# The opening of an S5 block rebuilt: B and C loaded in their natural layout and turned on TensorE, E built on GpSimd from early on, a second F group ahead of U, and the V loop taken two pairs at a time

## The reference

```
def s5_mixer(u, lam_re, lam_im, log_dt, b_re, b_im, c_re, c_im, d_skip, w_glu):
    ug = uf.reshape(bsz, seqlen, SSM_GROUPS, SSM_GROUP)
    dt = jnp.exp(log_dt.astype(f32))[:, None]
    mag = jnp.exp(lr * dt)
    ab_re = mag * jnp.cos(li * dt)
    ab_im = mag * jnp.sin(li * dt)
    ...
    coef_re = (nr * lr + ni * li) / den
    coef_im = (ni * lr - nr * li) / den
    bb_re = coef_re[..., None] * br - coef_im[..., None] * bi
    bb_im = coef_re[..., None] * bi + coef_im[..., None] * br
    bu_re = jnp.einsum('blgh,gph->blgp', ug, bb_re)
    bu_im = jnp.einsum('blgh,gph->blgp', ug, bb_im)
    ...
    _, _, xs_re, xs_im = lax.associative_scan(combine, (a_re, a_im, bu_re, bu_im), axis=1)
    y = (jnp.einsum('blgp,ghp->blgh', xs_re, c_re.astype(f32))
         - jnp.einsum('blgp,ghp->blgh', xs_im, c_im.astype(f32)))
    y = y.reshape(bsz, seqlen, D_MODEL) + d_skip.astype(f32) * uf
    y = jax.nn.gelu(y).astype(u.dtype)
    a, g = jnp.split(y @ w_glu, 2, axis=-1)
    return a * jax.nn.sigmoid(g)
```

## Time and profile before

| what | value |
|---|---|
| runs of the kernel before | 2005.61, 2001.52, 2005.14 us; median 2005.14 |
| span of the profiled execution | 1998.3 us |
| busy share of the span | PE 96%, VectorE 47%, ScalarE 38%, GpSimd 55% |
| chain that ended last | PE 86%, VectorE 6%, ScalarE 2%, GpSimd 2%, issue 2%, DMA 1%, SyncE 1% |
| costliest group | L2598, L2599, L2600 PE, gb<-xh,wh and the like, x1856 each, about 600 us each |
| w_ada blocks | 48 of 1 MB, median 5.5 us from issue to landing |

### The profile page before, as it was taken

The page is one execution under the profiler, slowest core; times in us unless marked ns, Lnnn a source line. Parts: engine busy times, 40 slices in busy tenths (PEclk is TensorE's granted clock), DMA queues, the critical chain, the costliest instruction groups (busy, mean ns, idle before and its releaser), DMA issues.

```text
span 1998.3 us, 31484 instructions
## 1 busy us (share of the span) xinstructions
PE 1912.5 (96%) x13077; PEld 1644.2 (82%) x13077; DVE 934.3 (47%) x1688; ACT 755.8 (38%) x1212; POOL 1108.0 (55%) x611
## 2 busy tenths in 40 slices
PE   8989999989999999899999999999999999989997
PEld 5578999878887788687778888888788988979997
DVE  7956641364935774732453111114386846372112
ACT  4343553332325422722323222222446435434443
POOL 6435997563535443343443444444468745757885
PEclk8999999989999999999999999999999999989999
DMA  6866776664122132124333323323634421655653
GB/s 165 239 215 225 256 230 219 239 216 156 62 76 64 33 126 64 32 64 137 127 107 126 95 79 121 104 63 110 209 116 128 159 85 54 204 196 174 189 173 98
DMA packets 289490, 276.60 MB, mean 138 GB/s; under 512 B 19802, under 2 KB 276324, under 8 KB 289092
## 3 DMA queue, kind: packets, MB, share of 16 engines
q1 hardware_dynamic: 286804, 271.42, 43.0%
q10 hardware_dynamic: 2192, 2.77, 0.4%
q0 software_dynamic: 352, 0.40, 0.1%
HBM read 266.70 MB, written 4.19 MB: 136 GB/s over the span
## 4 chain that ended last, share of the span: by engine, by line
PE 86%; DVE 6%; ACT 2%; POOL 2%; issue 2%; DMA 1%; SPq 1%; DVEq 0%; ACTq 0%; POOLq 0%
PE gb L2598 19%; PE gb L2599 18%; PE gb L2600 18%; PE gb L1757 3%; PE gb L1755 3%; PE gb L1756 3%; PE gb L1482 3%; PE gb L1483 3%; PE gb L1484 3%; POOL wl L2585 1%; PE mb L1208 1%; PE mb L667 1%; PE gb L667 1%; PE mb L1275 1%; DMA raw<-in_w_ada 1%
## 5 line engine op out<-in xcount | busy, mean ns | idle before, releaser
L2585 POOL TENSOR_TENSOR wl<-raw,wh 128x1024 fp32r<-128x1024 f32 (+3 forms) x448 | 977.8, 2201 | 797.0 <-ACT wh L819 796.7
L819 ACT CAST wh<-raw 128x1024 fp32r<-128x1024 f32 (+3 forms) x452 | 419.4, 937 | 680.8 <-PE gb L2600 399.7
L2598 PE MATMUL gb<-xh,wh 128*128 128x256 f32 (+1 forms) x1856 | 603.4, 325 | 11.0 <-DVE xl L1158 6.9
L2599 PE MATMUL gb<-xl,wh 128*128 128x256 f32 (+1 forms) x1856 | 599.5, 323 | 0.0
L2600 PE MATMUL gb<-xh,wl 128*128 128x256 f32 (+1 forms) x1856 | 599.4, 323 | 0.0
L2598 PEld LDWEIGHTS gb<-xh,wh 128*128 128x128 f32 x1856 | 351.8, 190 | 47.2 <-issue 14.6
L2600 PEld LDWEIGHTS gb<-xh,wl 128*128 128x128 f32 x1856 | 351.8, 190 | 27.6
L2599 PEld LDWEIGHTS gb<-xl,wh 128*128 128x128 f32 x1856 | 351.9, 190 | 27.2
L1755 PE MATMUL gb<-fhh,wh 128*128 128x512 f32 (+1 forms) x352 | 118.4, 336 | 0.0
L1757 PE MATMUL gb<-fhh,wl 128*128 128x512 f32 (+1 forms) x352 | 117.9, 335 | 0.0
L1756 PE MATMUL gb<-fhl,wh 128*128 128x512 f32 (+1 forms) x352 | 117.9, 335 | 0.0
(11 more groups left out here) (475 smaller groups left out, 3028.7 us busy)
## 6 DMA issues: line engine op xcount, KB each, us to landing
raw<-in_w_in SPq DMA_DIRECT2D x62, 1024.0 KB, 5.4
raw<-in_w_ada SPq DMA_DIRECT2D x48, 1024.0 KB, 5.5
raw<-in_w_ffn SPq DMA_DIRECT2D x44, 1024.0 KB, 5.2
raw<-in_mlp_w SPq DMA_DIRECT2D x32, 1024.0 KB, 5.6
raw<-in_w_ffn SPq DMA_DIRECT2D x16, 768.0 KB, 4.3
raw<-in_w_ffn SPq DMA_DIRECT2D x16, 640.0 KB, 4.1
raw<-in_ssm_w_glu SPq DMA_DIRECT2D x8, 1024.0 KB, 6.9
raw<-in_w_out SPq DMA_DIRECT2D x8, 1024.0 KB, 4.8
```

What stands on the lines that cost most here:

```text
L819: nc.scalar.copy(split_half(wh, p, j, h), raw_half(p, it, j, h)).then_inc(hi_ready, 1)
L2585: nc.gpsimd.tensor_tensor(split_half(wl, p, j, h), raw_half(p, it, j, h), split_half(wh, p, j, h).bitcast(F32), ALU.subtract)\
L2598: nc.tensor.matmul(o, H[:, k, :], XH, start=st, stop=False)
L2599: nc.tensor.matmul(o, H[:, k, :], XL, start=False, stop=False)
```

## The change

**Loads.** B comes by GpSimd's queue as two transfers of 32 partitions (`Bq`), C by SyncE's queue as two transfers (`cnat`). The gain, as 32 rows (`wq`), is made into diagonals (`wdiag`, one GpSimd operation of 32x1024), and 64 small products with them turn and weigh B at once, into PSUM banks 0 and 3. 32 small products turn C. x by chunk position is loaded to where the ring will be, so that the ring's first transfer waits for all eight copies of it in place of U's transposes.

**TensorE.** `warm(21)` becomes `warm(3)`; B, C, raw U, x in two halves, the vectors, `warm(3)`, w_ada blocks 0 and 1, the norm factor, blocks 2 and 3, then the loop. The loop handles two pairs per turn (16 turns), and holds six w_ada blocks in place of four, the first half of the K products (turn 9), the skip products and half of K's way back (turn 11). Twelve w_ada products in place of ten stand before y; those among y are at y3 and y5 (before: y0, y1, y3, y6).

**VectorE.** No product with the gain; F group 1 stands ahead of U; one `e_beside` in place of two, and no `e_last`, no `gate_lo`. **ScalarE.** Ct is copied between the two halves of x by group, two pairs' w1 in one copy. **GpSimd.** `wdiag` and `Db` early, E as soon as the powers and Ct are there, the chunk powers behind E's second quarter, seven halves of E in place of five, and all low halves of w_glu.

The core of the diff (pure moves of code and new buffer addresses are left out):

```diff
-        h32 = at("h32", [NCH, CH, D], F32, offset=arena1)[0]
-        xg = at("xg", [NCH, GROUPS, CH, GH], F32, offset=raw_at)[0]
-        xnat = at("xnat", [P, 2, D], F32, offset=toep_at)[0]
-        cnat = at("cnat", [P, 2, 4, P], F32, offset=toep_at + 8192)[0]
+        h32 = at("h32", [NCH, CH, D], F32, offset=raw_at)[0]
+        xg = at("xg", [NCH, GROUPS, CH, GH], F32, offset=toep_at)[0]
...
-        EARLY_ADA, EARLY_GLU = 10, 2
+        EARLY_ADA, EARLY_GLU = 12, 2
...
-                sp.wait_ge(s_U, 1)
+                sp.wait_ge(s_xg, CH)
...
-            sp.wait_ge(s_lnat, 16 * 3)
             xc = A["x"][0].rearrange("(c j) d -> j c d", j=CH)
-            for ri, name in enumerate(("ssm_b_re", "ssm_b_im")):
-                bn = A[name][0].rearrange("(q g) p h -> (g p) q h", g=2)
-                for r in range(2):
-                    sp.dma_start(Bn[:, ri, 16 * r:16 * r + 16, :], bn[:, 16 * r:16 * r + 16, :]).then_inc(s_Bn, 16)
-            rowg = A["norm_mix"][0].rearrange("(q g h) -> g q h", g=2, h=GH)
-            for g in range(2):
-                sp.dma_start(gain[64 * g:64 * g + 64, :, :], rowg[g].partition_broadcast(64)).then_inc(s_Bn, 16)
+            for ri, name in enumerate(("ssm_c_re", "ssm_c_im")):
+                sp.dma_start(cnat[:, ri, :, :], A[name][0].rearrange("(r g) h p -> (g h) r p", g=8)).then_inc(s_cnat, 16)
...
-            sp.wait_ge(s_ss, 1)
-            sp.wait_ge(s_ct5, 1)
+            sp.wait_ge(s_U, 1)
...
+            for j in range(4):
+                x_by_group(j)
...
+            act.wait_ge(s_ct5, 1)
+            act.wait_ge(s_vz, 2)
+            nc.scalar.copy(Ct[:, 0, :, 0:GH], gb[:, 1, :].rearrange("p (q h) -> p q h", h=GH)).then_inc(s_Ctc, 1)
+            nc.scalar.mul(Ct[:, 1, :, 0:GH], gb[:, 2, :].rearrange("p (q h) -> p q h", h=GH), -1.0).then_inc(s_Ctc, 1)
+            for j in range(4, CH):
+                x_by_group(j)
             act.wait_ge(s_xnat, 16)
+            act.wait_ge(s_Bt, 1)
...
-            act.wait_ge(s_xt, 1)
-            nc.scalar.copy(x[:, :, 0:SEQ], gb[:, :, :].rearrange("p b (k t) -> p (b k) t", k=2)).then_inc(s_x1, 1)
+            for i in range(2):
+                act.wait_ge(s_xt, i + 1)
+                nc.scalar.copy(x[:, 4 * i:4 * i + 4, 0:SEQ],
+                               gb[:, 1:3, :].rearrange("p b (k t) -> p (b k) t", k=2)).then_inc(s_x1, 1)
...
+            for b in range(PAIRS // 2):
+                act.wait_ge(s_w1t, b + 1)
+                if b >= 2:
+                    act.wait_ge(s_w1u, b - 1)
+                nc.scalar.copy(w1[:, 2 * (b % 2):2 * (b % 2) + 2, :, :],
+                               gb[:, 1 + b % 2, :].rearrange("p (a r m) -> p a r m", a=2, r=2)).then_inc(s_w1, 1)
+                if b % 4 == 0 and b:
+                    v_copy(b // 4 - 1)
+                if b == K_FIRST:
+                    kt_copy(0)
...
+            pool.dma_start(wq[:, :], A["norm_mix"][0].rearrange("(q n) -> q n", q=PAIRS)).then_inc(s_wq, 16)
+            for ri, name in enumerate(("ssm_b_re", "ssm_b_im")):
+                pool.dma_start(Bq[:, ri, :, :, :], A[name][0].rearrange("(q g) p h -> q g p h", g=2)).then_inc(s_Bq, 16)
...
+            pool.wait_ge(s_const, 16)
+            pool.wait_ge(s_wq, 16)
+            nc.gpsimd.tensor_tensor(wdiag[:, :, :, :].rearrange("q g h n -> q (g h) n"),
+                                    ident[0:PAIRS, 0:PAIRS].unsqueeze(1).to_broadcast([PAIRS, 2 * GH, PAIRS]),
+                                    wq[:, :].unsqueeze(2).to_broadcast([PAIRS, 2 * GH, PAIRS]), ALU.mult).then_inc(s_gd, 1)
+            nc.gpsimd.memset(sc[:, :, :], 0.0).then_inc(s_vz, 1)
+            nc.gpsimd.memset(zeros[:, :, :], 0.0).then_inc(s_vz, 1)
...
+            pool.wait_ge(s_pw, 1)
             pool.wait_ge(s_Ctc, 2)
-            pool.wait_ge(s_Bb, 1)
-            pool.wait_ge(s_U, 1)
             e_half(0, 0)
+            e_half(0, 1)
+            pool.sem_inc(s_E, 1)
             pool.wait_ge(s_th, 1)
             for s_ in range(2):
                 o = V_C + 8 * s_
                 pstep(g_.tensor_scalar(sc[:, :, 30 + s_], sc[:, :, 30 + s_], 0.5, 0.5, ALU.mult, ALU.add))
                 pstep(g_.tensor_tensor(sc[:, :, 30 + s_], sc[:, :, 30 + s_], vecs[:, o:o + 8], ALU.mult))
             pool.sem_inc(s_sc, 1)
-            e_half(0, 1)
-            pool.sem_inc(s_E, 1)
             e_half(1, 0)
             e_half(1, 1)
             pool.sem_inc(s_E, 1)
+            chunk_powers()
             e_half(2, 0)
+            e_half(2, 1)
+            pool.sem_inc(s_E, 1)
+            e_half(3, 0)
             pool.sem_inc(s_E, 1)
...
-                        if p is p_glu and it == 0 and j < EARLY_GLU:
-                            continue
-                        if p is p_glu and it == 0 and j == EARLY_GLU:
-                            pool.wait_ge(w_ready, 2 * EARLY_GLU)
...
-            warm(21, 3)
...
+            warm(3, 2)
+            pe.wait_ge(s_Bq, 16 * 2)
+            pe.wait_ge(s_gd, 1)
+            for ri in range(2):
+                for h in range(GH):
+                    for g in range(2):
+                        ins = nc.tensor.matmul(gb[64 * g:64 * g + 64, 3 * ri, PAIRS * h:PAIRS * h + PAIRS],
+                                               Bq[:, ri, g, :, h], wdiag[:, g, h, :], start=True, stop=True)
+            ins.then_inc(s_Bt, 1)
+            pe.wait_ge(s_cnat, 16 * 2)
+            of_parity = ident.rearrange("p (q g h) -> p g q h", q=4, g=2)
+            for ri in range(2):
+                for r in range(8):
+                    for g in range(2):
+                        ins = nc.tensor.matmul(gb[64 * g:64 * g + 64, 1 + ri, 64 * r:64 * r + 64],
+                                               cnat[:, ri, r, :], of_parity[:, g, :, :], start=True, stop=True)
+            ins.then_inc(s_ct5, 1)
...
+            pe.wait_ge(s_Ctc, 2)
+            pe.wait_ge(s_xnat, 16)
+            for i in range(2):
+                if i:
+                    pe.wait_ge(s_x1, 1)
+                for k in range(4):
+                    for a in range(2):
+                        ins = nc.tensor.transpose(gb[:, 1 + k // 2, (k % 2) * 256 + a * P:(k % 2) * 256 + a * P + P],
+                                                  xnat[:, a, (4 * i + k) * P:(4 * i + k) * P + P], ident)
+                ins.then_inc(s_xt, 1)
+            pe.wait_ge(s_vnat, 16 * NVEC)
+            pe.wait_ge(s_x1, 2)
+            for a in range(4):
+                ins = nc.tensor.transpose(gb[:, 1, a * P:a * P + P], vnat[:, a, :], ident)
+            ins.then_inc(s_vt, 1)
+            warm(3, 2)
+            pe.wait_ge(s_vc, 1)
+            pe.wait_ge(s_Bb, 1)
+            pe.wait_ge(s_sc, 1)
+            for n in range(2):
+                ada_block(pe, n)
             pe.wait_ge(s_small, 32)
             pe.wait_ge(s_chk, 1)
             for a in range(2):
+                ins = nc.tensor.matmul(gb[:, 1, GH * a:GH * a + GH], const[:, REP:CHK], chk[:, a, :], start=True, stop=True)
             ins.then_inc(s_fp5, 1)
+            for n in range(2, 4):
+                ada_block(pe, n)
+            pe.wait_ge(s_fac, 1)
...
+            pe.wait_ge(s_Uc, 1)
+            for b in range(PAIRS // 2 + 1):
+                if b == 12:
+                    for n in range(8, 10):
+                        ada_block(pe, n)
+                if b < PAIRS // 2:
+                    w1_transposes(b)
+                if b:
+                    v_products(b - 1)
+                if b in (2, 5, 7, 10):
+                    ada_block(pe, {2: 4, 5: 5, 7: 6, 10: 7}[b])
+                if b == K_FIRST:
+                    pe.wait_ge(s_Vc, 2)
+                    k_products(0)
+                if b == K_FIRST + 2:
+                    skip_products()
+                    k_back(0)
+            pe.wait_ge(s_w1, PAIRS // 2)
             k_products(1)
+            ada_block(pe, 10)
             k_back(1)
+            ada_block(pe, 11)
+            warm(8, 1)
...
-                late = ((0,), (1,), (), (2,), (), (), (3,), ())[d]
+                late = ((), (), (), (0,), (), (1,), (), ())[d]
...
-            dve.wait_ge(s_Bn, 16 * 6)
+            dve.wait_ge(s_Bt, 1)
+            Bn = [gb[:, 3 * ri, :].rearrange("p (h q) -> p q h", q=PAIRS) for ri in range(2)]
             cf = [sm[:, k, :].unsqueeze(2).to_broadcast([P, PAIRS, GH]) for k in (15, 17)]
-            cmul(Bb[:, 0, :, :], Bb[:, 1, :, :], Bn[:, 0, :, :], Bn[:, 1, :, :], cf[0], cf[1],
-                 tE[:, 0:PAIRS * GH].rearrange("p (q h) -> p q h", h=GH))
-            step(v.tensor_tensor(Bb[:, :, :, :], Bb[:, :, :, :],
-                                 gain[:, :, :].unsqueeze(1).to_broadcast([P, 2, PAIRS, GH]), ALU.mult))
+            cmul(Bb[:, 0, :, :], Bb[:, 1, :, :], Bn[0], Bn[1], cf[0], cf[1], tB[:, :, :])
...
+            f_group(1)
             dve.wait_ge(s_U, 1)
             dve.wait_ge(s_fac, 1)
             dve.wait_ge(s_sk, 1)
```

(15 more changed lines are left out.)

244 lines of the change are left out of this document (92 added, 152 removed).

## The result

| what | before | changed |
|---|---|---|
| median of 19 runs each | 2005.61 us | 2015.96 us |
| lowest and highest | 1999.95, 2010.2 | 2005.59, 2020.02 |
| ratio, 95% interval | | 1.0045, 1.0031 to 1.0058 |
| span of the profiled execution | 1998.3 | 2004.1 |
| first of the long products at | 124.6 | 128.1 |

The forecast was 2019.5 (1999 to 2026). The new runs split: four at 2005.6 to 2007.5, fifteen at 2011.2 to 2020.0. The profiled execution took 2005.88 and is one of the four, so its trace shows a mild form. By the same 1.8 the profiled execution of before (span 1998.3) took about 2000.1, my estimate, also at the low end of its kernel's 19 runs.

A forecast was written before the change was run, and what follows sets the result against it. TensorE, busy 96%, bounds the kernel, its long products starting at 124.6 us. Loop start +21, loop -4.6 and +8.0, y 17.5 later but 19.75 long: products at 139.2, +14.5, so 2019.5 against 2005.1; range 1999 to 2026.

The forecast's parts named there:

- largest term: VectorE's coefficients in the opening: six operations held by GpSimd's E, so that they end at 31 us, not at 20.
- the two waits that it blamed: GpSimd's E waited for U's transposes and Bb; without these waits E was to hold VectorE's operations before the scan.
- B's way: Start of the opening: spread-gain wait 1.69 and gain product 1.36 go, 3.05 us gained; B turned at 13 to 16.
- Powers: VectorE's opening: `wdiag` and two Db operations on GpSimd hold the powers, ending at 18 us (bounds 12 to 19.1).
- Coefficients: VectorE after the powers: E starts at 18 us too, six operations are held, ending at 31, not 20.
- rsqrt: VectorE behind F group 0: comes at 44.5, held by GpSimd's E, passes at about 55; about 8 us more.
- Loop: 16 turns of 1.15 us for 32 of 0.72: -4.6; added w_ada, K and skip work: +8.0; last V copy at 99.2.
- Scan to y: Between loop and y: scan and lags take 19.8 us to 119.2; y at 119.4, 17.5 later than before.
- y: Stage before the long products: 22.75 less 3.10 (w_ada wait) and 1.4 (clock), plus 1.5 (gelu holds), 19.75 us.
- C comes late: Rival: Ct copied at 20.5, coefficients pass before E; products at 122.2, 2003 us (2001 to 2006), chance 0.19.
- The clock falls within the loop: Rival: the loop's turns wait for ScalarE and the clock drops, up to 18.4 us more; chance 0.03.
- Sums: Opening's added instants: F group 0 at 44.5 from Bb at 36 and 8.1; F group 1 at 63.5 after rsqrt at 55.

The follow-up runs named there:

- e12: The changed kernel with GpSimd's E again waiting for Bb and U's transposes, silu(c) between its first halves: median 2014.3 us, 1.0045 of the kernel before.
- e1: The changed kernel run and profiled again, nothing altered: median 2012.1 us, 1.0049 of the kernel before.
- e7: The changed kernel with the four low halves of w_glu's first blocks back on VectorE: median 2012.8 us, 1.0036 of the kernel before.
- e6: The changed kernel with K's first half and way back, skip products and w_ada blocks 8 and 9 behind the loop: median 2012.7 us, 1.0043 of before.
- e2: The changed kernel with two GpSimd memsets moved behind the powers and Db's two products on VectorE behind F group 1: median 2019.8 us, 1.0068 of before.
- e9: The changed kernel with GpSimd's memsets behind the powers and Db's products behind silu(c): median 2010.3 us, 1.0025 of the kernel before.
- e3: The changed kernel with TensorE fillers, one more ahead of B and seven between C and U's transposes: median 2015.2 us, 1.0043 of the kernel before.
- e4: The changed kernel with the edits of e2 and e3 together: median 2024.3 us, 1.0086 of the kernel before.
- e10: The kernel of e9 with rsqrt's running values in PSUM and more TensorE fillers before the loop: median 2010.4 us, 1.0024 of the kernel before.
- e11: The kernel of e10 with e6's edit and three quarters of E's second half on VectorE: median 2005.0 us, 0.9999 of the kernel before.

## Why the prediction was right, and where its steps were not

The sign and the range were right, and so was the kind of cause: VectorE held by GpSimd. The place and the sizes were not. 14.5 us were forecast; the profile of 2005.9 shows 3.5 up to the products, the medians 10.4. That the forecast came as near as it did is in good part luck. Its path (`chk` at 55, U at 65.8, y at 119.4) occurs in no profile of the changed kernel's opening: `chk` came at 38.5 to 49.4, U at 50.1 to 60.1, and y at 105.8 to 113.1. Its largest term was absent in two of four, and e12, which puts back the two waits that it blamed, keeps the loss. Terms that it left out stood in their place.

- **B's way.** 13 to 16 was forecast, 17.2 measured: the 64 products took 7.31, above the 6.8 that was to be the upper bound. The 3.05 gained was never seen, since the coefficients came later than B.
- **Powers.** Bounds 12 to 19.1, taken 18, measured 20.1, outside. The two Db holds were there (2.36 and 2.35), but `wdiag` was priced alone, at 2.35: with three memsets it held one TENSOR_SCALAR for 4.37 us. Memsets were priced at nothing, and operations with one SBUF input were left out.
- **Coefficients.** "Six of these are held; they end at 31": in the first profile none was, Ct being copied at 21.9, beyond my bound of 20.5, and they end at 22.1. This step failed, and it is 9 us of the forecast path. It is a matter of chance: E began at 22.08 in the first profile and at 26.91 in e1, and no coefficient was held; it began at 21.36 in e7, and two were (3.5 us); at 21.18 in e6, and three were (5.7 us).
- **rsqrt.** "Comes at 44.5, passes at about 55", some 8 us of holds: in the first profile it came at 35.4 and found a gap. It was held for 3.8 us in e1 and, with `chk`, for 5.6 in e6, and also in e2, e9 and e12. So the mechanism is right, and the price of 8 too high.
- **The norm factor.** Not in my sum at all: silu(c) and w_ada stand ahead of it on TensorE, and most of what precedes them ran at half clock, so that it was ready at 47.7. Before it was ready at 38.4.
- **Loop.** Turn 1.15 forecast, 1.18 measured (transposes at 54.29, 55.47 and 56.64). Last V copy 3.4 us later than the loop's start would give; 5.8 measured. The excess is a wait of 1.77 us, since ScalarE copied K ahead of `w1`, and one for a w_ada block.
- **Scan to y.** 19.8 and y right behind the lags: 19.6 and 0.1.
- **y.** 19.75 forecast, 22.3 measured. The w_ada wait went as said. In its place stand waits of 0.59 and 1.97 us for held gelu operations, the longest 2.68, and the lower clock came back behind them (0.50 from 128 to 130, first products 0.21 us apart): 1.5 was priced, 2.6 and the clock of about 1.4 were found.
- **Rivals.** The first profile is the rival "C comes late", stage by stage: `chk` 37 forecast and 38.5 found, U 48 and 50.1, y 102.4 and 105.8; its sum missed the loop's and y's excess. Its ground, that TensorE "has little to do there, as in 31 to 37", misreads: TensorE was busy for 6.00 of those 6.00 us, with narrow products at 0.50. "The clock falls within the loop" had 0.03 and was seen in e2, e3, e4 and e6. Whether it lies behind the runs at 2016 to 2020 of the changed kernel was not seen, as none of those is profiled.
- **Sums.** F group 0 at 44.5 and F group 1 at 63.5 are each 0.4 over what their terms give (36 + 8.1, 55 + 8.1). Nothing hangs on it.

What the runs show of the cause: with GpSimd's early work out of the way about 4 to 6 of the 10 us come back (e9, e10), and all of it with K behind the loop and E shared as before on top (e11). What each of these parts is worth by itself, and what lengthens the rest of the program in some executions, stays open.

## What to carry to other kernels

Before work is moved to GpSimd, list what VectorE does beside it and whether its operands lie in PSUM; a small operation of the critical chain in SBUF costs as much as the GpSimd operation it meets, and when that meeting hangs on a landing DMA, the kernel can get a spread as well as a loss (`chk` at 38.5 to 49.4 in four profiles of one opening; e9 took 4 to 6 us back by order alone). Work moved out of a loop shortens the loop by its full length, but the path only up to the next thing that waits for that work (in e6 8 us in the loop, 2.7 up to y). Profile more than one execution before an instant is taken for the kernel's. Do not leave TensorE idle ahead of a chain of small matmuls: a gap of 6.5 us cost 5.7 more behind it, and fillers took that back.

## What was not expected of the hardware

- Memsets hold VectorE too, and single-input operations from SBUF to SBUF are held: a COPY of 0.27 us lasted 5.10, a TENSOR_SCALAR of 0.18 lasted 4.37, up to the end of the last of five GpSimd operations in a row. Not every VectorE operation is held so: L2941, with two inputs in SBUF, took its 0.18 us beside the first memset. The Trainium skill ("SBUF — State Buffer", section "SBUF: two separate sides") names operations in a two-port mode among those that lock against any GpSimd operation; these rows agree, if the two long ones ran in such a mode, which no row shows. I had used only its half on two SBUF inputs. The largest gap between GpSimd's five operations, 0.04 us, did not let the waiting one through.
- TensorE was busy with narrow matmuls from 9.9 to 20.8 us without a pause, and the granted clock of that stretch was 0.53 (B's 128 passes took 7.31 us); the V products, as narrow, ran at 1.00 in the loop from 50 to 70.
